# The last two steps of an expert loop in another order: first and third matrices of both pairs, then both second matrices

## What is computed

```
hb = silu(xb @ w1[e]) * (xb @ w3[e])     # w1, w3: 2048 x 512
y  = hb @ w2[e]                          # w2: 512 x 2048
out[token] += gate * y                   # then LN2(alpha * x + out)
```

## Time and profile before

| | us |
|---|---|
| median of three runs | 1283.78 |
| lowest and highest | 1280.99, 1285.2 |
| profiled execution, its own time | 1281.37 |
| span of the profiled execution | 1279.7 |
| PE busy in the span | 1233.4 (96%) |
| DVE busy | 444.8 (35%) |
| ACT busy | 319.3 (25%) |

### The profile page before, as it was taken

How to read it: one execution, slowest core, us unless ns; L and a number is a source line. 1 busy time by engine, 2 the same in 40 slices (tenths; PEclk the granted TensorE clock), 3 DMA queues, 4 the chain that set the end, 5 groups by cost and what they waited for, 6 DMA issues and landing times.

```text
span 1279.7 us, 15343 instructions
## 1 busy us (share of the span) xinstructions
PE 1233.4 (96%) x6669; PEld 710.7 (56%) x6669; DVE 444.8 (35%) x636; ACT 319.3 (25%) x544; POOL 7.1 (1%) x17
## 2 busy tenths in 40 slices
PE   6999999999999999999999999989998999989997
PEld 6989889988744444444444444445443444434433
DVE  7889996855410203133130211102020211111026
ACT  5443333533421211111211111111211111111212
POOL 1000000000000000000000000000000000000000
PEclk9999999999999999999999999999999999999998
DMA  8655555696999999999999999999999999999996
GB/s 310 217 186 188 171 191 184 234 383 222 351 389 422 418 423 427 425 427 428 428 428 428 426 429 428 427 427 428 428 427 428 428 428 429 427 427 428 423 411 236
DMA packets 71143, 472.28 MB, mean 369 GB/s; under 512 B 7978, under 2 KB 8562, under 8 KB 41762
## 3 DMA queue, kind: packets, MB, share of 16 engines
q1 hardware_dynamic: 70642, 470.48, 90.6%
q10 hardware_dynamic: 432, 0.79, 0.2%
HBM read 469.14 MB, written 2.10 MB: 368 GB/s over the span
## 4 chain that ended last, share of the span: by engine, by line
PE 78%; DMA 19%; DVE 2%; issue 0%; ACT 0%; SPq 0%; DVEq 0%; ACTq 0%
PE psum L912 30%; DMA ring<-in_w_dram 14%; PE psum L668 9%; PE psum L695 9%; PE psum L957 8%; PE psum L834 7%; DMA slot<-in_w_dram 5%; PE psum L624 5%; PE psum L627 2%; PE psum L870 2%; PE psum L871 2%; PE psum L992 1%; PE psum L899 1%; PE psum L811 1%; DMA area_a<-in_x_dram 1%; DVE area_b L1978 0%
## 5 line engine op out<-in xcount | busy, mean ns | idle before, releaser
L912 PE MATMUL psum<-ring,area_c 128*64 128x512 f32 x1424 | 386.8, 601 | 13.6 <-DMA ring<-in_w_dram 7.9
L912 PEld LDWEIGHTS psum<-ring,area_c 128*64 128x64 f32 x1424 | 120.9, 138 | 207.9 <-issue 204.7
L1279 ACT ACTIVATE area_c<-psum,gain 128x128 f32<-128x128 f32 x256 | 96.2, 456 | 294.7 <-PE psum L834 294.7
L1848 DVE TENSOR_TENSOR area_a<-area_a,psum 128x512 f32<-128x512 f32 x56 | 38.3, 683 | 354.6 <-PE psum L871 354.6
L1446 DVE TENSOR_TENSOR w_low<-ring,w_high 128x2048 fp32r<-128x2048 f32 x55 | 125.9, 2289 | 63.1 <-ACT w_high L1123 63.0
L1123 ACT ACTIVATE w_high<-ring 128x2048 fp32r<-128x2048 f32 x55 | 105.4, 1916 | 145.5 <-PE psum L627 42.5
L912 PE MATMUL psum<-slot,area_c 128*64 128x512 f32 x384 | 135.9, 599 | 0.0
L957 PE MATMUL psum<-ring,area_d 128*64 128x512 f32 x560 | 126.7, 594 | 4.5 <-DMA ring<-in_w_dram 4.5
L834 PE MATMUL psum<-one_hot,area_b 128*128 128x128 f32 x1024 | 124.9, 278 | 0.8 <-DVE one_hot L1775 0.8
L834 PEld LDWEIGHTS psum<-one_hot,area_b 128*128 128x128 f32 x1024 | 118.0, 192 | 13.1 <-issue 12.2
L1832 DVE TENSOR_TENSOR y_low<-psum,y_high 128x512 fp32r<-128x512 f32 x64 | 42.7, 686 | 235.8 <-ACT y_high L1288 235.8
(11 more groups left out here) (233 smaller groups left out, 1055.9 us busy)
## 6 DMA issues: line engine op xcount, KB each, us to landing
ring<-in_w_dram SPq DMA_DIRECT2D x101, 2048.0 KB, 29.7
slot<-in_w_dram SPq DMA_DIRECT2D x34, 2048.0 KB, 29.5
ring<-in_w_dram SPq DMA_DIRECT2D x46, 1024.0 KB, 10.2
ring<-in_w_in_dram SPq DMA_DIRECT2D x40, 1024.0 KB, 5.0
area_g<-in_w_dram SPq DMA_DIRECT2D x16, 2048.0 KB, 31.1
ring<-in_w_out_dram SPq DMA_DIRECT2D x16, 1024.0 KB, 5.2
slot<-in_w_dram SPq DMA_DIRECT2D x14, 1024.0 KB, 8.7
area_g<-in_w_dram SPq DMA_DIRECT2D x10, 1024.0 KB, 9.6
```

The lines of the kernel that those rows point to most:

```text
L912: mm = pe.matmul(psum[i * CAP:(i + 1) * CAP, j // UNITS, :], gathered[:, kk, i * CAP:(i + 1) * CAP], w[i][:, k, :], start=kk == 0, stop=kk ...
L1279: ins = act.activation(gathered[:, k, :], psum[:, 2 + g % 2, k % 4 * P:(k % 4 + 1) * P], ACT.Identity, scale=gain[:, 0, k:k + 1], bias=gai ...
L1848: v.tensor_tensor(area_a[:, 0, cols], area_a[:, 0, cols], psum[:, at, :], ALU.add)
```

## The change

The last two steps take another order: first and third of a, first and third of b, second of a, second of b. With it:

- SP loads the third matrices of b where the second of a stood, and the other way round. The sizes, the places and the number of DMAs stay as they were. The wide columns wait for units 4 and 5 of b, the narrow ones for units 6 and 7.
- TensorE does all eight units of b in one run. The transposes of b's one-hot table follow unit 4. The transposes of b's `hidden` lie between f = 1 and f = 2 of the second matrices of a.
- The combines of a, which lay in two pairs between the units of b, now lie one by one behind each f of `last_rows` for columns 0 and 1, in banks 0 to 3.
- ScalarE and VectorE do `hidden` of b first, then the handoffs of a.
- The rows of the last norm go to a place that is free earlier, and their wait is taken out.

```diff
-        PRODUCTS_DONE = (STEP_UNITS - 1) * (PAIRS - 2) + 4 * UNITS + FT - 1
+        PRODUCTS_DONE = (STEP_UNITS - 1) * (PAIRS - 2) + 4 * UNITS
-        ln2_slot = slots[slot_of(LATE + 4)]
+        ln2_slot = slots[slot_of(STEP_UNITS * PAIRS - 2 * SLOTS - PLACES)]
...
             for n in range(SLOTS - 2):
                 unit_used(PAIRS - 2, n)
-                if n < HALF // 2:
-                    load_expert_unit(LAST + n, n, PAIRS - 1)
-                else:
-                    load_expert_unit(LAST + n, n + UNITS, PAIRS - 2)
+                load_expert_unit(LAST + n, n, PAIRS - 1)
...
-            load_pair(LATE, STEP_UNITS - 2, PAIRS - 2)
+            load_pair(LATE, SLOTS - 2, PAIRS - 1)
             for j in range(0, UNITS, 2):
                 last_unit_used(j)
-                load_pair(LAST + SLOTS + j, UNITS + j, PAIRS - 1)
+                load_pair(LAST + SLOTS + j, 2 * UNITS + j, PAIRS - 2)
...
-            sp.wait_ge(y_ready, NC * (PAIRS - 1))
+            last_unit_used(SLOTS - 2)
...
-                sp.wait_ge(experts_done, PRODUCTS_DONE)
                 load_ln2_rows()
...
-                unit_products(b, b % TWO, lambda j: arrived(start + 2 * UNITS + j), False, units=range(UNITS))
-                for f in range(FT):
-                    hidden_rows(f, arrived(start + 3 * UNITS + f))
-                pe.wait_ge(silu_ready, PAIRS)
-                for t in range(TT):
-                    pe.transpose(psum[:, 0, t * P:(t + 1) * P], one_hot[:, b % TWO, t, :], ident[:])
-                pe.wait_ge(s_last_rows, 16 * 2)
-                pe.transpose(psum[:, 0, TT * P:TT * P + 2 * CT], last_rows_2,
-                             ident[0:2 * CT, 0:2 * CT]).then_inc(gt_ready, 1)
-                for j in range(UNITS, 2 * UNITS):
-                    unit_products(b, b % TWO, lambda j: arrived(start + 3 * UNITS + j), False, units=(j,))
-                    if j in (UNITS, 2 * UNITS - 1):
-                        first = 0 if j == UNITS else NC // 2
-                        combine(a, first)
-                        combine(a, first + 1)
+                for j in range(2 * UNITS):
+                    unit_products(b, b % TWO, lambda j: arrived(start + 2 * UNITS + j), False, units=(j,))
+                    if j == UNITS:
+                        pe.wait_ge(silu_ready, PAIRS)
+                        for t in range(TT):
+                            pe.transpose(psum[:, 0, t * P:(t + 1) * P], one_hot[:, b % TWO, t, :], ident[:])
+                        pe.wait_ge(s_last_rows, 16 * 2)
+                        pe.transpose(psum[:, 0, TT * P:TT * P + 2 * CT], last_rows_2,
+                                     ident[0:2 * CT, 0:2 * CT]).then_inc(gt_ready, 1)
+                for f in range(FT // 2):
+                    hidden_rows(f, arrived(start + 4 * UNITS + f))
...
                 mm.then_inc(ht_ready, 1)
+                for f in range(FT // 2, FT):
+                    hidden_rows(f, arrived(start + 4 * UNITS + f))
                 pe.wait_ge(half_kept, 1)
+                pe.wait_ge(ht_drained, PAIRS)
...
-                pe.wait_ge(comb_added, NC * b - 1)
+                pe.wait_ge(y_drained, NC * a + 2)
                 for f in range(FT):
-                    if f == FT // 2:
-                        pe.wait_ge(ht_drained, PAIRS)
                     for c in range(2):
                         last_rows(f, c, [wide[i][:, f, c, :] for i in range(2)], s_wide)
+                    combine(a, f, True)
...
-            for i in range(2):
-                add_combined(PAIRS - 2, 2 + i, COMBINED[i])
+            for c in range(0, NC, 2):
+                for i in range(2):
+                    keep_y_low(PAIRS - 2, c + i)
+                for i in range(2):
+                    add_combined(PAIRS - 2, c + i, 2 * i)
             more = dve.value_load(overflow[0:1, 0:1], min_val=0, max_val=1)
```

More of the change, by code:

```diff
@@ L859, in arrived_again, with combine @@
                 return [[slots[one % SLOTS][:, r * D:(r + 1) * D] for r in range(2)] for one in pair]
-            def combine(it, c):
+            def combine(it, c, beside=False):
                 if c == 0:
@@ L868, in combine @@
                 for t in range(TT):
-                    bank = COMBINED[c % 2] + t
+                    bank = (2 * (c % 2) if beside else COMBINED[c % 2]) + t
                     pe.matmul(psum[:, bank, :], one_hot_t[:, t, :], y_high[:, c % 2, :], start=True, stop=False)
@@ L1330, in halves @@
                     return ap.rearrange("p (f s) -> p f s", s=P)
[L1332 to L1337, removed]
+                act.wait_ge(gt_ready, PAIRS)
+                act.activation(last_gain, psum[:, 0, TT * P:TT * P + 2 * CT], ACT.Copy)
+                act.activation(one_hot_t_2[:], halves(psum[:, 0, 0:TT * P]), ACT.Copy).then_inc(gt_drained, 1)
                 act.wait_ge(half_turned, 1)
@@ L1342, in last_step @@
                                ACT.Copy).then_inc(ht_drained, 1)
+                for c in range(NC):
+                    keep_y_high(it - 1, c)
                 for c in range(NC):
@@ L1925, in _ @@
                         scaled_x1(it - LATE_ROWS)
-                if it == PAIRS - 1:
-                    for c in range(0, NC, 2):
-                        for i in range(2):
[L1929 to L1932, removed]
-                hide(it, it == PAIRS - 1)
-            for i in range(2):
-                add_combined(PAIRS - 2, 2 + i, COMBINED[i])
+                hide(it, it == PAIRS - 1)
+            for c in range(0, NC, 2):
[3 more added lines that the diff above has]
+                    add_combined(PAIRS - 2, c + i, 2 * i)
             more = dve.value_load(overflow[0:1, 0:1], min_val=0, max_val=1)
```

## The result

The changed kernel takes 1285.98 us, the median of 20 runs (1283.65 to 1287.78), the kernel before 1283.01 us (20 runs, 1280.99 to 1285.2). The ratio is 1.0020, 95% interval 1.0014 to 1.0026: slower by 1.8 to 3.3 us. Predicted were +3.0 us, 0.24%, and "within 0.3%".

What follows compares the result with a forecast made beforehand. The weight stream bounds the kernel until the last landing at 1239.2, then TensorE. Terms -9.74 + 12.00 + 0.20 + 0.06 + 0.20 + 0.33 = +3.05 us on 1283.78 give 1286.8 us, range 1283.0 to 1289.7.

Steps and rivals of the forecast that it cites:

- Place of the cost: From the last landing at 1239.2 TensorE bounds the kernel; work moved from before it to behind it is paid in full.
- One sign of being wrong: The forecast is wrong if the landing behind which the chain runs moves; it was expected again near 1239.
- -9.74: Old TensorE work after unit 7: two combines 1.97, transposes and copy wait 0.85, unbroken columns 0 and 1 6.92.
- the piece that lands last: First TensorE piece behind the last landing: 3.59 us, unit 7 before, f = 3 afterwards, no change.
- Four groups with single combines: Behind the last landing: four times eight matmuls (1.87) and a lone combine (1.13), together 12.00 us; low bound 11.0.
- the wait of 0.18: TensorE before the combine of a's column 2: VectorE's `y_low` takes 3.2 us against 3.00 of cover, wait 0.2.
- The first columns 2: First two f's of column 2, behind a combine: 1.87 us instead of 1.81, so 0.06 more.
- `value_load`: On VectorE between the adds of a's column 3 and b's `y_low`: 0.33 us, bounds 0 and 0.93.
- The clock: Rival: TensorE's 2.3 us idle before f = 3 of a lowers its clock, +4.7 us in all, chance 0.12.
- frequent short idles between groups: Part of the clock rival: alternating products and combines in the tail would cost one or more clock falls.
- The handoffs: Rival: handoffs before column 2's combine and b's first combine wait 1 us longer each, +5 us in all, chance 0.10.
- The transfers: Rival: late columns set the tail and moved combines are free, -0.9 to 0 us, chance 0.10.

## Why the prediction was right, point by point

**Place of the cost: right.** The last landing is that of f = 3 of step a, nothing ahead of it became late, and everything behind b's first combine kept its length. That was expected from the rows and is seen in the two profiles; that the combines are what is paid is shown by leaving half of them out. One sign of being wrong did turn up, the last landing 1.7 us later than 1239.2, but that shift lies ahead of the reordered loads.

**Terms.** Predicted were -9.74 + 12.00 + 0.20 + 0.06 + 0.20 + 0.33 = +3.05; the tail grew by 2.74. One by one: the piece that lands last took 3.56 us against 3.59. Four groups with single combines took 12.18 with one wait (1244.51 to 1256.69), which is 12.00 and the wait of 0.18 for which I had 0.20. The first columns 2 took 1.87 and a wait of 0.27, for which I had 0.20 of handoff and 0.33 of `value_load`. The one mis-sized term is `value_load`: 0.33 us predicted, nothing measured. The row of ScalarE that I took for it has a branch and a table load behind the value_load; it is no price of a `value_load` alone. The range had its zero. The medians differ by 2.97 us, nearly the +3.0 that was forecast. That closeness is luck: the sum has 0.3 us that nothing measured bears out, and the interval is 1.8 to 3.3.

**What I had not said.** I counted the 1.97 us of the second pair and the 0.85 of transposes and copy as what the kernel before pays behind unit 7. That is its longest path, but the adds of column 2 behind `hidden` are only 0.2 us shorter, and I did not name them. The sum came out the same, since both paths leave the tail together: `hidden` now lies ahead of the last landing, and TensorE no longer waits for that add. But 1.97 is not what the pair is worth alone (0.93 us less of it gained 0.22), and 0.85 is not what the new order gives back. That is the bare chain, 2.36. A prediction of the kernel with only the combines moved, made from the 0.85 us alone, would have been 17.88 + 0.85 = 18.7 us, 1.5 too low.

**The rivals.** The clock did not fall: over the changed kernel's stretch from before its transposes to its last combine the granted clock is 1.00 (stretch: us, busy of PE, PEld, DVE, ACT, POOL, clock, DMA share, GB/s):

```profile
1233.00:1270.70 37.70, 35.33 (x144) 13.14 (x140) 17.99 (x29) 6.72 (x11) 0.00 (x0) 1.00 0.82 321
```

The idle time ahead of the landing was 2.9 us in three pieces of at most 1.24. The Trainium skill ("TensorE: Matmul & The Clock Gate", "A second HAM failure mode: psum-queue depth-cycling") would have let frequent short idles between groups lower the clock. This tail, in which groups of products and combines alternate over all eight banks, shows no such fall; but it has only two idles between groups, of 0.17 and 0.27 us, and so is a weak test of that. The handoffs did fit under one f to within 0.2 to 0.3 us. The transfers do not set the tail: apart from the last landing, TensorE waits for none in it.

**SP.** The later wait of the wide columns and the removed wait cost nothing, as predicted: the columns' waits do not appear on the chain.

## What to carry to other kernels

Before a reordering, find the last landing and ask of each piece of work on which side of it it stands before and after. Work ahead of it, in a gap that ends at a landing, is free; behind it, it costs its full length, unless another path through the other engines ends at the same wait nearly as late. Then only the difference can be gained, until that path is shortened too. Such a path is easily missed: where an instruction waits for several semaphores and the engine that the row names had long been done, look in the program for the other waits. And where one engine hands buffers over in a fixed order of program, put the instruction for which another engine waits ahead of the one for which nobody waits.

## What the runs showed of the hardware

A `value_load` of VectorE between two instructions of 0.6 us cost no time (0.60 us from start to start with it, 0.59 without it). A combine of four matmuls with 512 columns costs 1.13 us between groups of another line, and 1.02 to 1.04 in a pair. And the stream of weights kept its pace to 0.1 us in 40 us with either order of the matrices, while its phase differed by up to 2.3 us between the profiled executions (last piece from 1239.26 to 1241.58).
